# A transformer block's dense expert gates in groups of eight expert tiles: the shape of one DRAM buffer

## The chip, the cores and the metric

The kernel runs on one core of a Trainium2 chip. The metric is the device time of one execution in microseconds (us); less is better. Engines: PE is TensorE (matmuls; PEld its weight loads), DVE is VectorE, ACT ScalarE, POOL GpSimd, SP SyncE. SP, ACT and POOL issue DMA transfers, each on a queue of its own (in the trace: q1 is SP's, q10 is ACT's, q0 POOL's gathers); all queues share the core's 16 DMA engines.

## The reference

One layer of a streaming encoder: 512 frames and 16 meta tokens, model width 1024, a layer norm, a joint projection, two mixers (sparse attention and an RWKV-7 scan), their gated join, and then PEER, the part that the change touches:

```python
q = (xf @ wq).reshape(n, PEER_HEADS, 2, PEER_HALF)
s = jnp.einsum('nhpd,hpkd->nhpk', q, subkeys)          # 8 heads, 2 halves, 128 keys each
s_top, i_top = lax.top_k(s, 16)
cand = s_top[:, :, 0, :, None] + s_top[:, :, 1, None, :]
best_s, best_j = lax.top_k(cand.reshape(n, PEER_HEADS, -1), 16)
expert = ...                                            # one of 128 * 128 experts for each pick
gate = jax.nn.softmax(best_s, axis=-1)
h = jnp.einsum('nd,nhkd->nhk', xb, u[eb])               # per token: 128 picked rows of u
coef = gb * jax.nn.gelu(h, approximate=False)
out = jnp.einsum('nhk,nhkd->nd', coef, v[eb])           # and of v
```

## The kernel before

The 16,384 experts are 128 tiles of 128. For 384 of the 512 tokens (`DENSE`) PEER is computed densely: all experts' activations `gelu(u x)`, times a dense gate matrix that is zero where an expert was not picked, times `v`. The other 128 tokens are done by gathers: POOL fetches 128 rows of `u` and 128 of `v` for each token (`gather_rows`, q0), and DVE takes dot products (`dot_rows`, L1552) and sums (`add_rows`, L1561), a few after each expert tile, by a fixed table `used_by`.

Work goes in this order on every engine:

1. Queries, scores and top-k, with expert tiles of `u` between them. Each tile of `u` is loaded by SP, split by ACT into a high part (L1855) and by DVE or POOL into the rest, multiplied on PE (`tile`, L1921 and L1925), passed through gelu by ACT (L1826) and, for the first 102 tiles (`PARKED`), stored to DRAM (`parked`, q10).
2. 24 lots (`LOTS`) of 16 tokens. In each lot PE runs two expert tiles and four groups of four tokens (`four`): one-hot matrices built by DVE, multiplied on PE (L1979), give the dense gates of four tokens for all 128 x 128 experts. ACT copies them (L1870) into `lot`, a buffer of two slots of 8 KB a partition: expert within the tile on the partition, then expert tile, then token. When four copies are there, SP stores the lot to `dense_gates` (L1758) and then issues the loads of the two weight tiles after the next (L1727).
3. Six more tiles (`BEHIND`), with no lots. Then SP waits until both of the last stores have landed (L1761), issues the first gates load (L1736), four loads of parked tiles (L1743), and the first three tiles of `v`.
4. For each expert tile k of 128: DVE multiplies the activations by the gates (`weigh`, L2170), ACT and DVE split the product (L1891, L2174), PE adds its product with `v` (`sums`, L2006). The first 102 activations are read back from `parked`; the last 26 are computed here from `u` (`hidden`). A gates load brings the gates of eight expert tiles (`LOOP`) into one of two slots; there are 16. Load 1 is issued at k = 1, load i + 1 at k = 8i + 5, once the first eight products of the slot have been read (`weighed`).
5. The last layer norm, by DVE, and the output.

SP issues its transfers in the order of the code, and they stand in one queue in that order: behind a store, the weight loads; behind a gates load, a parked tile and tiles of `v`. PE has two banks for the tiles' results in stages 2 and 3, so a gelu that is late holds up the tile after the next.

In the kernel before, `dense_gates` has the shape lot, partition, and 2048 numbers (expert tile and token). A store writes one lot, 8 KB a partition, in one piece. A gates load takes, for each partition and each of the 24 lots, 128 numbers (eight tiles by 16 tokens), 512 bytes.

Of the kernel before, what the change touches and what calls it, by code (L numbers as in the profile page):

```python
# [18 lines left out]
F32 = mybir.dt.float32  # L19
# [7 lines left out]
P = 128  # L27
# [14 lines left out]
EXPERT_KEYS, PEER_HEADS, PEER_TOPK = 128, 8, 16  # L42
LOT = 16
# [3 lines left out]
LOTS = DENSE // LOT  # L47
BETWEEN = 16
PARKED = 4 * PEER_HEADS + BETWEEN + 2 * LOTS + 6
GATHER_RING = 8  # L50
MARK, FILL, LOW = -3.4e38, -3.3e38, -1.0e30


# [63 lines left out]
def build(nc, a, out):  # L117

    with ExitStack() as ctx:
        def sb(name, shape, dt=F32, at=None):  # L120
            return (at or ctx).enter_context(nc.sbuf_tensor(name, shape, dt))

        def semaphore(name, at=None):
            return (at or ctx).enter_context(nc.semaphore(name))

        ps = ctx.enter_context(nc.psum_tensor("ps", [P, 8, 512], F32))
        params = sb("params", [P, NPARAM])
        ident = sb("ident", [P, P])
        ones = sb("ones", [P, P])
        pair_ones = sb("pair_ones", [P, P])  # L130
        h_tok = sb("h_tok", [P, NT, D])
        wi_tok = sb("wi_tok", [P, NT, HEADS])
        h1T = sb("h1T", [P, KD, SEQ])[:, :, :]

        flat_h1T = h1T.rearrange("p k t -> p (k t)")
        barred = [flat_h1T[:, 2 * D + sum(WIDTH[:i]):2 * D + sum(WIDTH[:i + 1])] for i in range(NT)]
        eps = sb("eps", [P, 4])

        dense = nc.dram_tensor("dense_gates", [LOTS, P, P * LOT], F32, kind="Internal").ap()
        gates_dram = nc.dram_tensor("branch_gates", [2 * KD, P, SEQ], F32, kind="Internal").ap()  # L140
        parked = nc.dram_tensor("parked_gelu", [PARKED, P, DENSE], F32, kind="Internal").ap()

        def par(name, i=0, rows=P):
            c = PCOL[name] + i
            return params[0:rows, c:c + 1]

        with ExitStack() as layer:

            arena = sb("arena", [P, CT_GATE * PW], at=layer)
            p_all = arena[:, :].rearrange("p (c t) -> p c t", c=CT_GATE)  # L150
            ab = sb("ab", [P, 2 * PAIRS, T], at=layer)
            out_gate = sb("out_gate", [P, PAIRS, T], at=layer)
            bonus = sb("bonus", [P, PAIRS, T], at=layer)
            chunk_decay = sb("chunk_decay", [P, PAIRS, 1 + SEQ // CHUNK], at=layer)
            attended_raw = sb("attended", [P, PAIRS * T], at=layer)[:, :]
            attended = attended_raw[:, 0:PAIRS * SEQ].rearrange("p (c t) -> p c t", c=PAIRS)
            masks = sb("masks", [P, 7, CHUNK], at=layer)
            project(nc, a, locals())
            attend(nc, a, locals())
            w_pa = sb("w_pa", [P, PAIRS, D], at=layer)  # L160
            scan_chunks(nc, a, locals())
            join(nc, a, locals())
        gather_sem = semaphores(nc, ctx, "gather")
        h_hl = sb("h_hl", [P, 2, KD, SEQ], F32R)
        rows_g = sb("gathered_rows", [P, GATHER_RING, D])
        gathering = {"rows": rows_g, "index": sb("pick_index", [P, PICKS], U32), "gate": sb("pick_gate", [P, PICKS]),
                     "hidden": sb("pick_hidden", [P, PICKS]), "picked": gather_sem("picked"), "used": gather_sem("used"),
                     "landed": [gather_sem(f"landed{j}") for j in range(GATHER_RING)]}
        peer(nc, a, locals(), out)


# [1363 lines left out]
def gather_rows(nc, pool, a, gathering, n):  # L1535

    slot = n % GATHER_RING
    if n >= GATHER_RING:
        pool.wait_ge(gathering["used"], n - GATHER_RING + 1)
    table = a["u_rows"] if n < PICKS else a["v"].rearrange("k p d -> (k p) d")  # L1540
# [24 lines left out]
def peer(nc, a, g, out):  # L1565


    ps, ident, h1T, h_hl, dense, parked = g["ps"], g["ident"], g["h1T"], g["h_hl"], g["dense"], g["parked"]
# [13 lines left out]
    RING = 4  # L1582
    BY_POOL = FIRST_LOT
    DEEP = 2 * RING
    LOOP, COEFS, HLS = 8, 4, 3
    TILES_D = DENSE // P
    FRESH = EXPERT_KEYS - PARKED
    LEAD = 2
# [53 lines left out]
    with ExitStack() as ctx:  # L1642
# [33 lines left out]
        with ExitStack() as second:  # L1676
            lot = sb("lot", [P, 2, P, LOT], at=second)
# [3 lines left out]
        with ExitStack() as third:  # L1681
            gates = sb("gates", [P, 2, LOTS, LOOP * LOT], at=third)
# [21 lines left out]
        lot_stored = [sem(f"lot_stored{j}") for j in range(2)]  # L1704
# [10 lines left out]
        @block.sync  # L1715
        def _(sp):
            def load(s, j):
                sp.dma_start(staged[:, j % RING, :], a["stream"][s]).then_inc(landed[j % RING], 16)

            def load_late(s):  # L1720

                j = place_of(s)
                if j < RING:
                    sp.wait_ge(late_low, before_in_place(s) - BY_POOL + 1)
                elif s >= QUERIES + PARKED + DEEP:
                    sp.wait_ge(late_low, s - DEEP - BY_POOL + 1)
                sp.dma_start(stage[j], source(s) if s >= QUERIES + PARKED else a["stream"][s]).then_inc(landed[j], 16)  # L1727

            def load_from(first, end):
                for s in range(first, min(end, STREAMED)):  # L1730
                    load_late(s)

            def load_gates(i):
                if i >= 2:
                    sp.wait_ge(weighed, LOOP * (i - 1))
                sp.dma_start(gates[:, i % 2], dense[:, :, LOOP * LOT * i:LOOP * LOT * (i + 1)].rearrange("l p k -> p l k")  # L1736
                             ).then_inc(gates_landed[i % 2], 16)

            def load_parked(k):
                if k >= COEFS:  # L1740
                    sp.wait_ge(coef_low, k - COEFS + 1)
                sp.wait_ge(act_parked[k % 2], 16 * (k // 2 + 2))
                sp.dma_start(coef[k % COEFS], parked[k]).then_inc(act_landed[k % COEFS], 16)  # L1743

            for j in range(RING):
                load(j, j)
            sp.dma_start(g_row, a["ln1_g"].partition_broadcast(P)).then_inc(rows_landed, 16)
            sp.dma_start(b_row, a["ln1_b"].partition_broadcast(P)).then_inc(rows_landed, 16)
            sp.dma_start(sub_keys[:, :, :], a["sub_keys"]).then_inc(keys_landed, 16)
            with sp.Fori(0, BY_POOL // 8) as i:  # L1750
                for j in range(8):
                    sp.wait_ge(w_low, i * 8 + (j + 1))
                    load(i * 8 + (j + RING), j)
            for n in range(LOTS):
                first = FIRST_LOT + TILES_A_LOT * n + RING
                load_from(first, min(first + TILES_A_LOT, QUERIES + PARKED))
                sp.wait_ge(four_copied, 4 * (n + 1))
                sp.dma_start(dense[n], lot[:, n % 2, :, :].rearrange("p k n -> p (k n)")).then_inc(lot_stored[n % 2], 16)  # L1758
            load_from(FIRST_BEHIND + RING, QUERIES + PARKED)
            for j in range(2):  # L1760
                sp.wait_ge(lot_stored[j], 16 * (LOTS // 2))  # L1761
            load_gates(0)
            for k in range(COEFS):
                load_parked(k)

            load_from(QUERIES + PARKED, QUERIES + PARKED + 3)
            for j in range(2):
                sp.wait_ge(act_parked[j], 16 * (PARKED // 2 + 1))
            load_from(QUERIES + PARKED + 3, QUERIES + PARKED + DEEP)
            for k in range(EXPERT_KEYS):  # L1770
                if k + LEAD in U_AT:
                    load_from(U_AT[k + LEAD] + DEEP, U_AT[k + LEAD] + DEEP + 1)
                load_from(V_AT[k] + DEEP, V_AT[k] + DEEP + 1)
                if k == 1:
                    load_gates(1)
                if k % LOOP == LOOP - 3 and LOOP < k < EXPERT_KEYS - LOOP:
                    load_gates(k // LOOP + 1)
                if k + COEFS < PARKED:
                    load_parked(k + COEFS)
            sp.wait_ge(late_low, STREAMED - BY_POOL)  # L1780
            sp.dma_start(g2_row, a["ln2_g"].partition_broadcast(P)).then_inc(row_landed, 16)
            sp.dma_start(b2_row, a["ln2_b"].partition_broadcast(P)).then_inc(row_landed, 16)
            for t in range(NT):
                sp.wait_ge(ready, t + 1)
                sp.dma_start(out[0, P * t:P * (t + 1), :], h_tok[:, t, :]).then_inc(stored, 16)
            sp.wait_ge(stored, 16 * NT)
# [499 lines left out]
```

## Time and profile before

| | |
|---|---|
| three executions | 2085.87, 2084.53, 2076.84 us, median 2084.53 |
| profiled execution | 2081.93 us, its span 2080.2 us |
| granted TensorE clock, mean | 0.957 of full speed |
| busy, share of the span | PE 92%, DVE 74%, ACT 37%, POOL 28% |
| DMA | 416.53 MB in 173,719 packets, 200 GB/s on average |
| `dense_gates` stores | 24 of 1024 KB, issued from 1080.4 to 1338.7 us |
| gates loads | 16 of 1536 KB, issued from 1344.1 to 1954.7 us |

All times in the trace are from the span's start. The span is a little shorter than the execution's time, which also holds what lies around it. Busy shares over the whole span mix stages with different limits; the rows further down are therefore taken by stretches. The DMA share is the mean busy share of the 16 DMA engines; it can pass 1.00 a little, since a packet's time overlaps with its neighbour's. A packet is one contiguous piece.

### The profile page before, as it was taken

How to read it: one execution, taken by the hardware profiler on the slowest of the kernel's cores; microseconds unless marked ns; L12 is line 12 of the kernel's file. 1: busy time of each engine (PE TensorE's matmuls, PEld its weight loads, DVE VectorE, ACT ScalarE, POOL GpSimd, SP SyncE). 2: the span in 40 equal slices, each digit the busy share in tenths (PEclk: the TensorE clock that was granted, in tenths of full speed). 3: DMA queues.
4: the chain of work that ended last, by engine and by line, in shares of the span. 5: the costliest groups of instructions: out<-in, count | busy, mean ns of one | idle time of the engine just before them, and what ended most of it. 6: DMA issues, size and time to landing. Idle time of an engine off the chain costs nothing.

```text
span 2080.2 us, 34092 instructions
## 1 busy us (share of the span) xinstructions
PE 1909.4 (92%) x13250; PEld 1617.5 (78%) x13250; DVE 1537.8 (74%) x2826; ACT 761.0 (37%) x1113; POOL 581.0 (28%) x403
## 2 busy tenths in 40 slices
PE   5989998789999879999999999969999999999892
PEld 4968876348974359999999999958888788888782
DVE  6277993314545269999978888748877788799998
ACT  3222554532210033333446666523333333332320
POOL 2322343000000035555531011222222222266661
PEclk9988998897999999999999999989999999999997
DMA  3211232010023034344567777899999999999994
GB/s 124 71 61 47 86 111 71 0 42 3 4 79 126 0 146 138 131 132 134 172 234 277 267 272 267 307 322 361 339 364 344 345 346 349 312 356 389 382 347 152
DMA packets 173719, 416.53 MB, mean 200 GB/s; under 512 B 13952, under 2 KB 89216, under 8 KB 170384
## 3 DMA queue, kind: packets, MB, share of 16 engines
q1 hardware_dynamic: 119728, 256.16, 36.0%
q0 software_dynamic: 36864, 134.23, 17.2%
q10 hardware_dynamic: 16992, 24.26, 3.2%
q8 instruction: 95, 1.56, 0.3%
q14 instruction: 40, 0.33, 0.1%
HBM read 363.08 MB, written 51.51 MB: 199 GB/s over the span
## 4 chain that ended last, share of the span: by engine, by line
PE 34%; DVE 24%; DMA 4%; issue 2%; SPq 0%; ACT 0%; DVEq 0%; ACTq 0%
PE ps L2006 18%; PE ps L1921 8%; DVE h_tok L1561 7%; PE ps L1925 4%; PE ps L1979 3%; DVE w_hl L2144 2%; DVE is_place L2088 2%; DVE is_place L2083 1%; DVE picks L2091 1%; DVE top_at L2049 1%; DVE top_at L2058 1%; DVE s_head L2052 1%; DMA coef<-parked_gelu 1%; DMA gates<-dense_gates 1%; DMA h1T<-in_v 1%
## 5 line engine op out<-in xcount | busy, mean ns | idle before, releaser
L2006 PE MATMUL ps<-w_hl,coef_hl 128*128 128x512 f32 x2304 | 539.1, 394 | 28.3 <-DVE coef_hl L2174 28.3
L2006 PEld LDWEIGHTS ps<-w_hl,coef_hl 128*128 128x128 f32 x2304 | 432.9, 189 | 130.5 <-DVE coef_hl L2174 37.0
L1921 PE MATMUL ps<-h_hl,w_hl 128*128 128x384 f32 (+1 forms) x2304 | 446.6, 345 | 19.9 <-ACT h1T L1826 11.1
L1921 PEld LDWEIGHTS ps<-h_hl,w_hl 128*128 128x128 f32 x2304 | 406.4, 189 | 33.2 <-ACT w_hl L1855 11.4
L1542 POOL DMA_INDIRECT gathered_rows<-in_u_rows,pick_index x128 | 137.5, 1074 | 538.2 <-DVE pick_hidden L1552 529.2
L1925 PE MATMUL ps<-h_hl,w_hl 128*128 128x384 f32 (+1 forms) x1152 | 230.0, 340 | 0.0
L1855 ACT ACTIVATE w_hl<-w_staged 128x1024 fp32r<-128x1024 f32 x143 | 152.0, 1063 | 188.9 <-PE ps L2006 137.2
L1925 PEld LDWEIGHTS ps<-h_hl,w_hl 128*128 128x128 f32 x1152 | 203.4, 188 | 5.0
L1542 POOL DMA_INDIRECT gathered_rows<-in_v,pick_index x128 | 164.8, 1288 | 148.4 <-DVE h_tok L1561 97.9
L1795 POOL TENSOR_TENSOR w_hl<-w_staged,w_hl 128x1024 fp32r<-128x1024 f32 x64 | 163.7, 2561 | 135.5 <-ACT w_hl L1820 111.1
L1561 DVE SCALAR_TENSOR_TENSOR h_tok<-gathered_rows,pick_hidden,h_tok 128x1024 f32<-128x1024 f32 x128 | 164.1, 1282 | 10.0 <-DVE h_tok L1561 0.5
L632 PE MATMUL ps<-hT_hl,w_hl 128*128 128x264 f32 (+1 forms) x1024 | 168.1, 323 | 0.0
L2144 DVE TENSOR_TENSOR w_hl<-w_staged,w_hl 128x1024 fp32r<-128x1024 f32 x130 | 157.8, 1218 | 11.2 <-ACT w_hl L1855 11.2
L297 POOL TENSOR_TENSOR w_hl<-w_staged,w_hl 128x1024 fp32r<-128x1024 f32 x40 | 102.8, 2571 | 213.6 <-ACT w_hl L480 213.6
L632 PEld LDWEIGHTS ps<-hT_hl,w_hl 128*128 128x128 f32 x1024 | 150.6, 198 | 14.4 <-issue 2.8
L1552 DVE CUSTOM_DVE_ANT_0 gathered_rows<-gathered_rows,h_tok 128x1024 f32<-128x1024 f32 x128 | 155.4, 1217 | 0.0
L1855 ACT ACTIVATE w_hl<-h1T 128x1024 fp32r<-128x1024 f32 x78 | 82.9, 1063 | 169.2 <-PE ps L2006 125.8
L2174 DVE TENSOR_TENSOR coef_hl<-coef,coef_hl 128x384 fp32r<-128x384 f32 x128 | 71.2, 556 | 73.4 <-ACT coef_hl L1891 73.1
L1891 ACT ACTIVATE coef_hl<-coef 128x384 fp32r<-128x384 f32 x128 | 65.6, 513 | 142.1 <-DVE coef L2170 141.7
L1790 POOL IOTA count<- 128x16 f32 x1 | 0.1, 148 | 397.7 <-POOLq L111 397.7
L1826 ACT ACTIVATE h1T<-ps 128x384 f32<-128x384 f32 x102 | 50.0, 491 | 155.9 <-PE ps L1925 152.1
L2144 DVE TENSOR_TENSOR w_hl<-h1T,w_hl 128x1024 fp32r<-128x1024 f32 x78 | 94.5, 1217 | 16.4 <-ACT w_hl L1855 16.4
(315 smaller groups left out, 2546.8 us busy)
## 6 DMA issues: line engine op xcount, KB each, us to landing
w_staged<-in_stream SPq DMA_DIRECT2D x132, 512.0 KB
h1T<-in_v SPq DMA_DIRECT2D x66, 512.0 KB
w_staged<-in_v SPq DMA_DIRECT2D x62, 512.0 KB
dense_gates<-lot SPq DMA_DIRECT2D x24, 1024.0 KB
gates<-dense_gates SPq DMA_DIRECT2D x16, 1536.0 KB
w_staged<-in_w_in_t SPq DMA_DIRECT2D x40, 512.0 KB
parked_gelu<-h1T ACTq DMA_DIRECT2D x102, 192.0 KB
coef<-parked_gelu SPq DMA_DIRECT2D x102, 192.0 KB
```

Of the source, the lines that this page charges most:

```text
L297: nc.gpsimd.tensor_tensor(w_hl[:, j, 1, :], w_staged[:, j, :], w_hl[:, j, 0, :].bitcast(F32), ALU.subtract).then_inc(w_low, 1)
L632: nc.tensor.matmul(banks[b], w_hl[:, j, 0, P * k:P * (k + 1)], hT_hl[:, part, k, lo:hi], start=(k == 0 and part == 0), stop=False)
L1542: nc.gpsimd.indirect_dma_start(gathering["rows"][:, slot, :], None, table, bass.IndirectOffsetOnAxis(gathering["index"][:, column:column + ...
L1552: nc.vector.tensor_tensor_reduce(rows, rows, h_tok[:, 0, :], 1.0, 0.0, ALU.mult, ALU.add, gathering["hidden"][:, n:n + 1]).then_inc(gather ...
L1561: nc.vector.scalar_tensor_tensor(h_tok[:, 0, :], gathering["rows"][:, slot, :], gathering["hidden"][:, pick:pick + 1], h_tok[:, 0, :], ALU ...
L1795: nc.gpsimd.tensor_tensor(w_hl[:, j % RING, 1, :], staged[:, j % RING, :], w_hl[:, j % RING, 0, :].bitcast(F32), ALU.subtract).then_inc(w_ ...
L1855: nc.scalar.activation(w_hl[:, s % RING, 0, :], stage[place_of(s)], ACT.Copy).then_inc(w_high, 1)
L1921: nc.tensor.matmul(ps[:, bank, 0:width], w_hl[:, j % RING, 0, P * k:P * (k + 1)], h_hl[:, part, k, lo:SEQ], start=(k == 0 and part == 0), ...
L1925: last = nc.tensor.matmul(ps[:, bank, 0:width], w_hl[:, j % RING, 1, P * k:P * (k + 1)], h_hl[:, 0, k, lo:SEQ], start=False, stop=(k == KD ...
L2006: last = nc.tensor.matmul(ps[:, 2 + 2 * t + half, :], coef_hl[:, k % HLS, c, P * t:P * (t + 1)], w_hl[:, s % RING, v, 512 * half:512 * (ha ...
L2144: v_.tensor_tensor(w_hl[:, s % RING, 1, :], stage[place_of(s)], w_hl[:, s % RING, 0, :].bitcast(F32), ALU.subtract).then_inc(late_low, 1)
L2174: v_.tensor_tensor(coef_hl[:, k % HLS, 1, :], coef[k % COEFS], coef_hl[:, k % HLS, 0, :].bitcast(F32), ALU.subtract).then_inc(coef_low, 1)
```

## The change

The buffer `dense_gates` gets another shape: group of eight expert tiles, partition, lot, and 8 x 16 numbers. A gates load then reads 24 x 128 numbers, 12 KB, in one piece for each partition. A store writes a lot as 16 pieces of 512 bytes for each partition, 1.5 MiB apart in DRAM; in SBUF its source stays as it is. Sizes, the order of instructions on every engine, waits and semaphores are the same; `LOOP` keeps its value of 8 and is now named by a constant of the module.

```diff
+GATE_TILES = 8
...
-        dense = nc.dram_tensor("dense_gates", [LOTS, P, P * LOT], F32, kind="Internal").ap()
+        dense = nc.dram_tensor("dense_gates", [EXPERT_KEYS // GATE_TILES, P, LOTS, GATE_TILES * LOT], F32, kind="Internal").ap()
...
-    LOOP, COEFS, HLS = 8, 4, 3
+    LOOP, COEFS, HLS = GATE_TILES, 4, 3
...
             def load_gates(i):
                 if i >= 2:
                     sp.wait_ge(weighed, LOOP * (i - 1))
-                sp.dma_start(gates[:, i % 2], dense[:, :, LOOP * LOT * i:LOOP * LOT * (i + 1)].rearrange("l p k -> p l k")
+                sp.dma_start(gates[:, i % 2], dense[i]
                              ).then_inc(gates_landed[i % 2], 16)
...
                 sp.wait_ge(four_copied, 4 * (n + 1))
-                sp.dma_start(dense[n], lot[:, n % 2, :, :].rearrange("p k n -> p (k n)")).then_inc(lot_stored[n % 2], 16)
+                sp.dma_start(dense[:, :, n, :].rearrange("g p c -> p g c"),
+                             lot[:, n % 2, :, :].rearrange("p (g k) n -> p g (k n)", k=LOOP)).then_inc(lot_stored[n % 2], 16)
```

## Rows read from the trace of the kernel before

**Rows 1.** The page: busy time of the engines, and the chain that ended last.
```profile
PE 1909.4 (92%) x13250; PEld 1617.5 (78%) x13250; DVE 1537.8 (74%) x2826; ACT 761.0 (37%) x1113; POOL 581.0 (28%) x403
...
PE 34%; DVE 24%; DMA 4%; issue 2%; SPq 0%; ACT 0%; DVEq 0%; ACTq 0%
```

**Rows 2.** Stretches: us, busy of PE, PEld, DVE, ACT, POOL, PEclk, DMA share, GB/s.
```profile
1080.00:1339.00 259.00, 259.00 (x2214) 251.77 (x2213) 225.09 (x368) 159.84 (x186) 30.43 (x26) 1.00 0.78 271
1344.00:1360.00 16.00, 13.91 (x81) 13.59 (x79) 6.94 (x10) 2.88 (x4) 6.46 (x5) 1.00 1.06 370
1360.00:1372.00 12.00, 2.96 (x9) 2.99 (x10) 3.45 (x6) 3.60 (x5) 0.81 (x1) 0.60 0.84 315
1372.00:1400.00 28.00, 21.12 (x86) 17.06 (x86) 16.51 (x27) 7.34 (x11) 6.22 (x6) 0.93 0.89 303
1440.00:1480.00 40.00, 40.00 (x177) 32.81 (x176) 31.47 (x48) 13.59 (x20) 9.69 (x10) 1.00 1.00 351
1860.00:1920.00 60.00, 55.57 (x272) 48.40 (x272) 57.70 (x56) 19.54 (x27) 37.78 (x29) 1.00 1.02 380
```

**Rows 3.** PE's timeline: start, duration, engine, line, tiles, count [idle before <- releaser].
```profile
1353.58 2.93 PE L1921 MATMUL ps<-h_hl,w_hl 128*128 128x384 f32 x16
...
1369.04 4.67 PE L1921 MATMUL ps<-h_hl,w_hl 128*128 128x384 f32 x16 [11.13 <-ACT h1T L1826]
...
1386.39 18.55 PE L2006 MATMUL ps<-w_hl,coef_hl 128*128 128x512 f32 x72 [4.77 <-DVE coef_hl L2174]
1405.45 6.92 PE L2006 MATMUL ps<-w_hl,coef_hl 128*128 128x512 f32 x29 [0.51 <-DVE coef_hl L2174]
...
1649.91 2.34 PE L2006 MATMUL ps<-w_hl,coef_hl 128*128 128x512 f32 x9 [1.09 <-DVE coef_hl L2174]
```

**Rows 4.** ACT's timeline, same columns, 1340 to 1390 us.
```profile
1367.46 1.06 ACT L1855 ACTIVATE w_hl<-h1T 128x1024 fp32r<-128x1024 f32 x1 [15.94 <-DMA h1T<-in_v]
1368.43 0.47 ACT L1826 ACTIVATE h1T<-ps 128x384 f32<-128x384 f32 x1
```

**Rows 5.** SP's queue in order of time, 1320 to 1420 us.
```profile
1327.40 0.33 SPq L1758 DMA_DIRECT2D dense_gates<-lot  x1
...
1338.66 0.33 SPq L1758 DMA_DIRECT2D dense_gates<-lot  x1
...
1344.15 0.38 SPq L1736 DMA_DIRECT2D gates<-dense_gates  x1
1344.57 11.94 SPq L1743 DMA_DIRECT2D coef<-parked_gelu  x4
1356.55 23.69 SPq L1727 DMA_DIRECT2D h1T<-in_v  x4
```

**Rows 6.** DMA queue 1, 1354 to 1356 us: packets, MB, share of 16 engines.
```profile
q1 hardware_dynamic: 1097, 0.56, 108.8%
```

**Rows 7.** DMA queue 1, 1366 to 1368 us.
```profile
q1 hardware_dynamic: 221, 0.82, 102.7%
```

**Rows 8.** DMA packets in all, by size, and queue 1, 1283 to 1287 us.
```profile
DMA packets 173, 1.17 MB, mean 292 GB/s; under 512 B 16, under 2 KB 16, under 8 KB 45
...
q1 hardware_dynamic: 173, 1.17, 95.0%
```

**Rows 9.** DMA queue 10 (parked tiles' stores), 1370 to 1372 us.
```profile
q10 hardware_dynamic: 163, 0.23, 32.0%
```

**Rows 10.** ACT's rows in the timeline, 1282 to 1312 us.
```profile
1300.47 1.06 ACT L1855 ACTIVATE w_hl<-w_staged 128x1024 fp32r<-128x1024 f32 x1 [1.17 <-DMA w_staged<-in_stream]
...
1302.01 0.49 ACT L1826 ACTIVATE h1T<-ps 128x384 f32<-128x384 f32 x1 [0.48 <-PE ps L1925]
```

**Rows 11.** DMA queue 0 (the gathers), 1348 to 1352 us.
```profile
q0 software_dynamic: 349, 1.27, 78.2%
```

**Rows 12.** DMA queues 0 and 1, 1360 to 1362 us.
```profile
q0 software_dynamic: 180, 0.63, 81.6%
q1 hardware_dynamic: 182, 0.16, 23.2%
```

## The prediction

> **What bounds the kernel now.** The order of reading is: the page's totals and its chain of waits, the stretches, and then, where TensorE (PE) stands still, the timelines of the engines and the DMA queues. The span is 2080.2 us and PE is busy for 92% of it; the chain ends on PE and VectorE (DVE) lines, and DMA holds 4% of it [rows 1]. That small share is all that a change of transfers alone can reach directly, so the question is where it lies. The stretches tell [rows 2]. While the dense gates are made and stored (1080 to 1339 us) PE is busy all the time, and the 16 DMA engines for 0.78 of it. From 1400 to about 1800 PE is full too (40.00 of 40), although DMA stands at 1.00. From 1860 on DVE is the bound (57.70 of 60 us) and PE merely waits for it. Only 1344 to 1405 us holds an open stall: PE works 13.91 of 16, 2.96 of 12 and 21.12 of 28 us.
>
> The PE timeline names these stalls [rows 3]: 11.13 us before the tile at 1369.04, 4.77 before the sums at 1386.39, 0.51 at 1405.45, and one later of 1.09 at 1649.91, while a gates load is awaited. Behind the first is ScalarE (ACT), which waits 15.94 us for the first tile of `in_v` and only then, at 1368.43, can apply the gelu that frees PE's bank [rows 4]. Behind that is SyncE's (SP's) queue [rows 5]: the last store of dense gates is issued at 1338.66, the first gates load at 1344.15, when both store semaphores are up, then four loads of parked tiles, whose issue takes 11.94 us in all, and so the first `in_v` load leaves at 1356.55. Its bytes are behind the whole gates load in one queue.
>
> **The change, part by part.** No instruction is added, removed or moved on any engine. Each of 16 gates loads goes from 3,072 pieces of 512 bytes to 128 pieces of 12 KB; each of 24 stores goes from 128 pieces of 8 KB to 2,048 of 512 bytes. All transfers use 16 DMA engines, so per engine a load falls from 192 pieces to 8, and a store rises from 8 to 128.
>
> *Price of a load.* In 1354 to 1356 only gates pieces run on queue 1: 1,097 packets take 108.8% of 2 us on 16 engines, 34.8 engine-us, 31.7 ns for one [rows 6]. A load costs 192 x 31.7 = 6.1 us of all engines. A 4 KB piece costs, from 1366 to 1368, 32.9 engine-us for 0.82 MB, about 200 pieces, 0.164 us [rows 7]; a 12 KB piece at this rate is 0.49 us and the load 8 x 0.49 = 3.9 us. The saving is 2.1 us of DMA a load.
>
> *Price of a store.* From 1283 to 1287 one store and the start of a weight load take 95.0% of 4 us on 16 engines, 60.8 engine-us, for 1.17 MB [rows 8]. Of its packets 45 are under 8 KB and 16 of these under 512 bytes, so 29 are weight pieces of 4 KB; at 0.164 us each [rows 7] they leave 0.44 us for each of the 128 pieces, 8 x 0.44 = 3.5 us a store. The trace has no write of 512 bytes to memory. Bounds: a 512-byte read, 31.7 ns [rows 6], makes 128 x 31.7 = 4.1 us; the parked tiles' writes of 1,536 bytes, which take 32.0% of 2 us on 16 engines, 10.2 engine-us, for 0.23 MB, about 150 pieces, so 68 ns each [rows 9], make 8.7 us. At the other side a rate as that of large pieces, 20 ns for 512 bytes, would make 2.6 us, a gain of 0.9. I take 4.1, since the read has the same size and the written 1,536 bytes cost hardly more per byte than a 4 KB read. So a store costs 0.6 us more.
>
> *What the stores cost.* In a lot of 11.26 us (from 1327.40 to 1338.66 [rows 5]) DMA is busy for 0.78, which leaves 2.5 us; 0.6 fits. Behind the store in the queue stand two weight loads, and ACT waits 1.17 us for the first of them; the gelu behind it has still 0.48 us in hand before PE's tile is ready, and the bank it frees is wanted only by the tile after the next, over 5 us later [rows 10]. A delay of 0.6 us costs nothing; what hides it is this spare bank, and were it gone, 24 x 0.6 = 14 us would show. The last store has no such cover: the gates load waits for it, and all behind moves by 0.6 us.
>
> *What the loads gain.* At 1344 to 1368: 2.1 us less in front of the `in_v` tile, less 0.6 from the late store, is 1.5 us. Turns matter too: when the gathers (queue 0) compete, from 1348 to 1352 they hold 78.2% of the engines [rows 11], and from 1360 to 1362 the queues pass as many packets (180 and 182) while queue 0 holds 81.6% of the time [rows 12]. So a queue with 512-byte pieces gets small turns, and with 12 KB pieces large ones. But the turns won in the gates load are given back: the four parked loads after it have pieces of 1,536 bytes (32 turns an engine, each against a gather piece of 0.17 us), and the gathers put off then run beside them. Of 8 turns of the `in_v` tile itself perhaps half a microsecond is won. I take 2.0 us for the first stall. The 4.77 us stall follows it one to one, as it waits for the parked gelus of the same tiles, and keeps its length. The stall of 0.51 us (a parked load behind the second gates load) and that of 1.09 us go: 1.6 us. The other gates loads lie beside full PE or beside a full DVE and give nothing. Sum: 2.0 + 1.6 = 3.6 us. Bounds of the first stall's gain: from -3.1 us (the last store at 8.7 us, 5.2 late, less the 2.1) to all of 11.13.
>
> The profiled execution took 2081.93 us, its sum 2078.3; it lies 2.6 us under the median of 2084.53, from which the same sum gives **2080.9**. A measurement of this kernel can tell about 0.5%, 10.4 us, from no change, and 3.6 us is well inside: I forecast no difference that shows.
>
> **Rivals.** *The stall disappears.* If queue 1 gets far more turns than counted, or the parked loads are issued so much sooner that the gathers fall behind them, the `in_v` tile is there 11 us earlier. Then 11.13 us go, and with it the slow start after it: the 16 matmuls at 1369.04 take 4.67 us where a running PE takes 2.93 for the same (the granted clock was 0.60 in this stretch [rows 2], against 1.00 elsewhere), 1.7 us. With the 1.6 us above: 14.4 us, 2070.1 us. For it: SP's issue is held up 11.94 us by the many pieces [rows 5]. Against it: the bytes before the tile stay, and the engines are busy for 1.06 and 0.84 of the stretches before it [rows 2].
>
> *The stores become the bound.* If a written piece costs more than (3.5 + 2.5) / 128 = 47 ns, a lot has more DMA work than its 11.2 us, the weights come late, and PE waits in all 24 lots. At the upper bound of 68 ns it is 8.7 - 6.0 = 2.7 us a lot, 65 us in all, 2150 us. For it: the profile shows no such small write, and 1,536 bytes already took 68 ns. Against it: time per packet grows with bytes in every row.
> A rule speaks for this rival. In this trace the old loads, whose successive pieces lie 1 MiB apart, already move 512 bytes in 31.7 ns [rows 6], against 20 ns for 512 bytes at the rate of 4 KB pieces [rows 7]; which part of the 11 ns is the small piece's and which the distance's, no row tells. The Trainium skill (DMA: Bandwidth & Descriptors, section on latency and other measured facts) reports that copies between tensors with a row pitch of a large power of two fall from 207 to 164 GB/s at 2 MiB and to 103 at 4 MiB; the new stores step 1.5 MiB between a partition's pieces. The trace has no such halving at its 1 MiB step. If a new piece took twice the 31.7 ns, by the same working, it would be 8.1 us a store, 2.1 us over, 50 us in all and 2135 us; I give this cause 0.04 of the 0.10 below.
>
> *All is hidden.* The gathers take up what the loads release, and the store's delay eats the rest: 2084.5 us. It differs from my forecast in size only. That the pieces are cut smaller than 12 KB is possible too and ends at the same place.
>
> **How the numbers follow.** Forecast of a few microseconds: 0.52. Nothing at all: 0.16. The stall gone or most of it: 0.22. Slow stores: 0.10. The first two are within 0.5%; of the third nearly all counts as faster, a part of it, where only half the stall goes, does not. Thus faster 0.21, within 0.5% 0.69, slower 0.10. The range goes from 2067 (the stall gone from a median as shown, and 3 us for the runs' own spread) to 2091 (no gain, a late store, and the spread of the runs); the slow stores are outside it.
>
> **What would show it.** Right: a gates load that holds the engines for about 3.9 us, not 6.1; lots still 11.2 us apart; PE full to 1339 us; the stall near 1369 about 9 us long; no stall at a gates load. The first rival: that stall under 3 us and a clock of 1.00. The second: PE stalls in the lots with ACT waiting for `w_staged`, DMA at 1.0 from 1080 to 1339. Wrong outright: a change of the time after 1860 us, where I count none.

## The result, and the profile after

The changed kernel takes 2139.32 us (median of 4, 2135.93 to 2140.72) against 2083.34 us: a ratio of 1.0271, 95% interval 1.0244 to 1.0299. The prediction, 2080.9 us with a range of 2067 to 2091 and 0.69 on "within 0.5%", is wrong. It is slower by 56 us, where the forecast saw 3.6 us of gain.

The page after, in the lines that answer to [rows 1], and its packets:

```profile
PE 1940.8 (91%) x13250; PEld 1636.7 (77%) x13250; DVE 1537.4 (72%) x2826; ACT 756.9 (35%) x1113; POOL 578.5 (27%) x403
...
DMA packets 172695, 416.53 MB, mean 195 GB/s; under 512 B 13952, under 2 KB 89216, under 8 KB 170384
...
PE 27%; DVE 23%; DMA 8%; issue 3%; ACT 2%; SPq 0%; ACTq 0%; DVEq 0%
```

The bytes are the same, and the count of packets hardly differs: what the loads lost in small pieces the stores gained. DMA's part of the chain has doubled from 4% to 8%.

The spans differ by 58.8 us. Laid out by the stores of dense gates: the first store is issued at 1087.74 us, 7.3 later than before; the 24 stores take 303.9 us from first to last (before: 1080.42 to 1338.66, 258.2), 45.6 more; and from the last store to the end it is 747.4 us (741.5), 5.9 more. The first part is not put down to the change: nothing ahead of the first store differs, and in the other profiled executions its time runs from 1075.3 to 1085.6. The last part is not put down to late transfers either. Its main row on PE, before and after:

```profile
L2006 PE MATMUL ps<-w_hl,coef_hl 128*128 128x512 f32 x2304 | 539.1, 394 | 28.3 <-DVE coef_hl L2174 28.3
```

```profile
L2009 PE MATMUL ps<-w_hl,coef_hl 128*128 128x512 f32 x2304 | 547.4, 399 | 27.1 <-DVE coef_hl L2177 27.1
```

The same 2,304 matmuls take 8.3 us more, though PE waits no longer than before and the granted clock is 1.00 in the steady stage of both. Run 3 below has the same transfers in this stage, and there they take 539.0 us, so the new shape of the buffer does not do it; why this execution was slower there stays open. What is the change's is the loss in the lots, 45.6 us of the 56.

Stretches of the kernel after, in the columns of [rows 2]:

```profile
1088.00:1146.00 58.00, 58.00 (x493) 56.43 (x492) 50.63 (x83) 33.98 (x40) 5.67 (x5) 1.00 0.80 261
1146.00:1392.00 246.00, 217.63 (x1741) 209.48 (x1741) 173.74 (x283) 121.48 (x145) 20.50 (x21) 0.95 0.70 226
...
1460.00:1500.00 40.00, 40.00 (x173) 32.42 (x172) 31.98 (x50) 13.29 (x18) 9.52 (x10) 1.00 0.94 331
...
1920.00:1980.00 60.00, 55.52 (x270) 48.19 (x269) 57.60 (x56) 18.95 (x26) 37.70 (x29) 1.00 1.00 393
```

For the first five lots PE is still full. Then it stands still for 28 of 246 us. Its work there also takes some 14 us more than at the pace before (1,741 matmuls in 217.63 us, where 2,214 took 259.00): the granted clock was 0.95 in this stretch, where it was 1.00. These two are most of the 45.6 us. And the DMA engines are busy for less of the time (0.70) than before the change (0.78), so they have time to spare. The later stages are as forecast but for the slower matmuls: PE full, DMA down from 1.00 to 0.94, and DVE the bound at the end, 57.60 of 60 us.

Who waits in the lots, 1088 to 1392 us (engine, line, releaser: us in total, times, longest):

```profile
ACT w_hl L1858 <- DMA w_staged<-in_stream: 122.9, 23, 7.2
PE ps L1924 <- ACT h1T L1829: 28.4, 15, 4.0
```

ACT waits once a lot for weights, 5.3 us on average, where it waited about 1 us. Two lots in SP's queue, an early and a late one:

```profile
1099.11 0.38 SPq L1760 DMA_DIRECT2D dense_gates<-lot  x1
...
1110.76 0.38 SPq L1760 DMA_DIRECT2D dense_gates<-lot  x1
...
1282.61 0.38 SPq L1760 DMA_DIRECT2D dense_gates<-lot  x1
1283.04 3.07 SPq L1729 DMA_DIRECT2D w_staged<-in_stream  x2
1296.01 0.38 SPq L1760 DMA_DIRECT2D dense_gates<-lot  x1
```

and the same two lots on ACT:

```profile
1106.85 1.06 ACT L1858 ACTIVATE w_hl<-w_staged 128x1024 fp32r<-128x1024 f32 x1 [2.31 <-DMA w_staged<-in_stream]
...
1292.11 1.06 ACT L1858 ACTIVATE w_hl<-w_staged 128x1024 fp32r<-128x1024 f32 x1 [5.86 <-DMA w_staged<-in_stream]
1293.08 0.47 ACT L1829 ACTIVATE h1T<-ps 128x384 f32<-128x384 f32 x1
...
1293.96 2.02 ACT L1873 ACTIVATE lot<-ps 128x512 f32<-128x512 f32 x2 [0.41 <-ACT h1T L1829]
```

Read the late lot as a circle: store at 1282.61, the two weight loads behind it in the same queue, the first of them in ACT's hands at 1292.11 (9.5 us after the store), then ACT's split, gelu and two copies, and with the fourth copy the next store, at 1296.01 (3.9 us). A lot takes 9.5 + 3.9 = 13.4 us, whatever PE could do. This sum holds in every lot of the changed kernel: the first part goes from 7.5 to 10.8 us, and the next store is issued 3.9 us after it each time. Before the change the first part was 6.2 to 6.9 us (6.75 in the lot of [rows 10], whose store was issued at 1293.72), so the circle needed 10.1 to 10.8 us and PE's pace of 11.2 ruled. The first part may be 11.2 - 3.9 = 7.3 us long. In the early lot it is 7.7.

PE in the late lot, with its stall, and the same sixteen matmuls when PE had not stood still (4.58 us against 3.02; seven of the 15 stalls were followed by such slow ones):

```profile
1293.69 4.58 PE L1924 MATMUL ps<-h_hl,w_hl 128*128 128x384 f32 x16 [1.96 <-ACT h1T L1829]
...
1300.86 3.02 PE L1924 MATMUL ps<-h_hl,w_hl 128*128 128x384 f32 x16
```

### The profile page after: what moved, and what is told of

It is laid out like the page before. It is cut to its first block, busy times and chain, and to the rows that moved or that the text cites. A ratio compares the mean times of both kernels' runs of the same rounds, so it can differ in the third digit from the quotient of the medians.

```text
span 2139.0 us, 34092 instructions
## 1 busy us (share of the span) xinstructions
PE 1940.8 (91%) x13250; PEld 1636.7 (77%) x13250; DVE 1537.4 (72%) x2826; ACT 756.9 (35%) x1113; POOL 578.5 (27%) x403
## 4 chain that ended last, share of the span: by engine, by line
PE 27%; DVE 23%; DMA 8%; issue 3%; ACT 2%; SPq 0%; ACTq 0%; DVEq 0%
PE ps L2009 20%; DMA w_staged<-in_stream 7%; DVE h_tok L1563 7%; PE ps L1924 4%; DVE w_hl L2147 2%; PE ps L1928 2%; DVE is_place L2091 1%; DVE is_place L2086 1%; DMA h1T<-in_v 1%; PE ps L1982 1%; ACT lot L1873 1%; DVE picks L2094 1%; DVE top_at L2052 1%; DVE top_at L2061 1%; DVE s_head L2055 1%
## 5 line engine op out<-in xcount | busy, mean ns | idle before, releaser
L2009 PE MATMUL ps<-w_hl,coef_hl 128*128 128x512 f32 x2304 | 547.4, 399 | 27.1 <-DVE coef_hl L2177 27.1
L1924 PE MATMUL ps<-h_hl,w_hl 128*128 128x384 f32 (+1 forms) x2304 | 459.5, 352 | 48.5 <-ACT h1T L1829 39.7
L1924 PEld LDWEIGHTS ps<-h_hl,w_hl 128*128 128x128 f32 x2304 | 418.5, 195 | 65.2 <-ACT w_hl L1858 42.7
L1928 PE MATMUL ps<-h_hl,w_hl 128*128 128x384 f32 (+1 forms) x1152 | 230.1, 340 | 0.0
L1928 PEld LDWEIGHTS ps<-h_hl,w_hl 128*128 128x128 f32 x1152 | 203.6, 188 | 5.0
L1563 DVE SCALAR_TENSOR_TENSOR h_tok<-gathered_rows,pick_hidden,h_tok 128x1024 f32<-128x1024 f32 x128 | 164.2, 1283 | 10.0 <-DVE h_tok L1563 0.5
L2147 DVE TENSOR_TENSOR w_hl<-h1T,w_hl 128x1024 fp32r<-128x1024 f32 x78 | 94.6, 1219 | 13.7 <-ACT w_hl L1858 13.7
L1873 ACT ACTIVATE lot<-ps 128x512 f32<-128x512 f32 x96 | 97.0, 1117 | 20.0 <-ACT h1T L1829 14.5
```

The costliest lines, as they stand in the source:

```text
L1563: nc.vector.scalar_tensor_tensor(h_tok[:, 0, :], gathering["rows"][:, slot, :], gathering["hidden"][:, pick:pick + 1], h_tok[:, 0, :], ALU ...
L1873: nc.scalar.activation(lot[:, n % 2, :, FOUR * q:FOUR * (q + 1)].rearrange("p k n -> p n k"), ps[:, 4 + q, :].rearrange("p (n k) -> p n k" ...
L1924: nc.tensor.matmul(ps[:, bank, 0:width], w_hl[:, j % RING, 0, P * k:P * (k + 1)], h_hl[:, part, k, lo:SEQ], start=(k == 0 and part == 0), ...
L1928: last = nc.tensor.matmul(ps[:, bank, 0:width], w_hl[:, j % RING, 1, P * k:P * (k + 1)], h_hl[:, 0, k, lo:SEQ], start=False, stop=(k == KD ...
L2009: last = nc.tensor.matmul(ps[:, 2 + 2 * t + half, :], coef_hl[:, k % HLS, c, P * t:P * (t + 1)], w_hl[:, s % RING, v, 512 * half:512 * (ha ...
L2147: v_.tensor_tensor(w_hl[:, s % RING, 1, :], stage[place_of(s)], w_hl[:, s % RING, 0, :].bitcast(F32), ALU.subtract).then_inc(late_low, 1)
```

## Experiments

The theories that went in. **A**: the circle just read. **B**: the distance of 1.5 MiB between a partition's pieces makes the writes slow. **C**: the DMA engines have no time left in a lot, the rival on record. Ratios are to the kernel before on the same chip.

**1. Small pieces both ways, stored side by side.**

```diff
-        dense = nc.dram_tensor("dense_gates", [EXPERT_KEYS // GATE_TILES, P, LOTS, GATE_TILES * LOT], ...)
+        dense = nc.dram_tensor("dense_gates", [EXPERT_KEYS // GATE_TILES, LOTS, P, GATE_TILES * LOT], ...)
...
-                sp.dma_start(gates[:, i % 2], dense[i]
+                sp.dma_start(gates[:, i % 2], dense[i].rearrange("l p c -> p l c")
...
-                sp.dma_start(dense[:, :, n, :].rearrange("g p c -> p g c"),
+                sp.dma_start(dense[:, n, :, :].rearrange("g p c -> p g c"),
```

> Stores in 512-byte pieces as in the change, but their pieces for neighbouring partitions lie side by side in 64 KB blocks, and the gates loads are back at 512-byte pieces. Theory A (a circle: a lot's store stands in SP's queue ahead of the two weight loads; ACT waits for the first of these before its gelu and the copies that release the next store): nothing changes in the lots, periods of 13.3 to 13.8 us, total 2130 to 2145. Theory B (the 1.5 MiB between a partition's pieces makes the writes slow): the distance is gone, so the lots come back to 11.3 us and the total to 2080 to 2090. Theory C (the 16 DMA engines have no time left in a lot): as A here.

Measured: 2127.58 us, ratio 1.0227 (1.0188 to 1.0267). First to last store 302.5 us, against 303.9. B falls: it asked for 2080 to 2090. The total is 2.4 us under the range of A and C (2130 to 2145); the lots start at 11.4 us, are over 13 from the eighth on and reach 14.9. Its ratio is 0.0044 under the changed kernel's, some 9 us, with nearly the same time in the lots; the slower matmuls read above are as large, and here they take 539.5 us. The price of the distance, too, can be read: queue 1 in 1283 to 1287 us, first of the changed kernel, where only store pieces run, then of this one:

```profile
q1 hardware_dynamic: 1752, 0.90, 80.9%
```

```profile
q1 hardware_dynamic: 699, 0.36, 30.8%
```

The share times 16 engines times 4 us gives 51.8 engine-us for 1,752 packets, 29.6 ns each, and 19.7 for 699, 28.2 ns. Here a 512-byte write costs about as much as the 512-byte read of [rows 6] (31.7 ns), near or far.

**2. Large pieces both ways.** The loads read 12 KB runs of the old buffer, which hold gates of other experts and tokens; the right gates are left out, the work is the same.

```diff
+            by_load = dense.rearrange("l p k -> (l p k)").rearrange("(i p c) -> i p c", p=P, c=LOTS * LOOP * LOT)
...
-                sp.dma_start(gates[:, i % 2], dense[:, :, LOOP * LOT * i:LOOP * LOT * (i + 1)].rearrange("l p k -> p l k")
+                sp.dma_start(gates[:, i % 2].rearrange("p l k -> p (l k)"), by_load[i]
```

> Stores of 8 KB a partition as before, and gates loads of 12 KB a partition from the same buffer; DVE multiplies by gates that belong to other experts and tokens. It measures the loads' half of the change alone. A, B and C all say that the lots stay at 11.26 us; the record's sum gives the loads 5.6 us before the late store is taken off (4.1 at the first stall, 1.6 at the two small ones at most), so 2076 to 2083. If 12 KB pieces themselves do harm by holding up gathers and weights, over 2087.

Measured: 2075.85 us, ratio 0.9974 (0.9954 to 0.9994). The lots stay at 11.2 us, and from the last store to the end it takes 736.1 us instead of 741.5: 5.4 us. The expectation had 2076 to 2083. The sum on record without its late store is 2.0 + 0.6 + 1.6 = 4.2 us (the expectation added it up wrongly, to 5.6). The loads' half of the change is of the sign and size that was forecast; the loss in the lots comes with the stores. The parts of the sum are not those forecast:

```profile
1363.96 5.46 PE L1923 MATMUL ps<-h_hl,w_hl 128*128 128x384 f32 x16 [7.62 <-ACT h1T L1828]
...
1379.80 16.76 PE L2008 MATMUL ps<-w_hl,coef_hl 128*128 128x512 f32 x72 [0.66 <-DVE coef_hl L2176]
1398.84 21.35 PE L2008 MATMUL ps<-w_hl,coef_hl 128*128 128x512 f32 x92 [2.27 <-DVE coef_hl L2176]
```

The first stall is 3.5 us shorter, the one of 4.77 us, which was to stay, has 0.66 left, the one of 0.51 us, which was to go, is 2.27, and the matmuls behind the first stall are slower than before.

**3. The weights ahead of the store.** Only SP's order changes: the two loads that used to be issued right behind a store are issued right ahead of it. Pieces and bytes stay those of the changed kernel.

```diff
+            load_from(FIRST_LOT + RING, FIRST_LOT + RING + TILES_A_LOT)
             for n in range(LOTS):
...
-                load_from(first, min(first + TILES_A_LOT, QUERIES + PARKED))
                 sp.wait_ge(four_copied, 4 * (n + 1))
+                load_from(first + TILES_A_LOT, first + 2 * TILES_A_LOT)
                 sp.dma_start(dense[:, :, n, :].rearrange("g p c -> p g c"),
...
-            load_from(FIRST_BEHIND + RING, QUERIES + PARKED)
```

> The changed kernel, but SP issues the two weight loads ahead of the lot's store, not behind it; the same pieces and bytes. A: the circle is cut, lots 11.2 to 11.4 us, PE full to the end of the lots, total 2074 to 2086. B and C: the writes take as long and the engines have the same work, so the lots stay at 13 us or more, total over 2125.

Measured: 2078.92 us, ratio 0.9978 (0.9955 to 1.0001). The stretch of its lots:

```profile
1078.00:1337.00 259.00, 259.00 (x2215) 251.77 (x2214) 224.52 (x367) 156.16 (x184) 32.14 (x27) 1.00 0.84 273
```

PE is full, with the same small pieces and more DMA work in the same time (0.84). A had 2074 to 2086, B and C over 2125. This carries the verdict: A holds, and C is out. The slower store does harm only where the awaited loads stand behind it.

**4. Each lot stored twice, in large pieces, in the kernel before.**

```diff
                 sp.dma_start(dense[n], lot[:, n % 2, :, :].rearrange("p k n -> p (k n)")).then_inc(lot_stored[n % 2], 16)
+                sp.dma_start(again[n % 2], lot[:, n % 2, :, :].rearrange("p k n -> p (k n)")).then_inc(lot_stored[n % 2], 16)
```

(the waits on `lot_stored` count twice as far; `again` is a new DRAM buffer that nothing reads.)

> The kernel before, each lot stored twice in 8 KB pieces, the second time to a buffer that nothing reads. No small piece anywhere. A: the weights land 3.5 us later, a period of 6.4 + 3.5 + 3.9 = 13.8 us once the slack is used, total 2125 to 2145. C: DMA work of 0.78 * 11.26 + 3.5 = 12.3 us a lot, 24 * 1.0 = 25 us, total 2105 to 2112. B, or any theory in which the small pieces as such do the harm: 2082 to 2090.

Measured: 2172.76 us, ratio 1.0428 (1.0389 to 1.0467); a miss on the far side of A, 28 us over its range. No piece is small, and the lots are the slowest of all: 14.3 to 15.7 us from the third on, the last but one 16.4. From SP's and ACT's timelines and the stretch of its lots:

```profile
1304.14 0.33 SPq L1759 DMA_DIRECT2D dense_gates<-lot  x1
```

```profile
1314.59 1.06 ACT L1857 ACTIVATE w_hl<-w_staged 128x1024 fp32r<-128x1024 f32 x1 [6.82 <-DMA w_staged<-in_stream]
```

```profile
1084.00:1423.00 339.00, 283.01 (x2232) 272.54 (x2231) 224.34 (x367) 154.40 (x185) 24.75 (x25) 0.94 0.75 280
```

The first part is 10.4 us in this lot, and 10.4 + 3.9 is 14.3. The circle is there without small pieces. But the weights came later than the 3.5 us added: A lacked something, which is run 5's question.

**5. No gathers in the lots.** In the changed kernel the gather's issue moves against the store from lot to lot. POOL's timeline, an early and a late lot (stores at 1099.11 and 1282.61):

```profile
1102.44 1.13 POOL L1544 DMA_INDIRECT gathered_rows<-in_u_rows,pick_index  x1 [10.09 <-DVE pick_hidden L1554]
```

```profile
1282.45 0.94 POOL L1544 DMA_INDIRECT gathered_rows<-in_u_rows,pick_index  x1 [12.39 <-DVE pick_hidden L1554]
```

```diff
                 low(BY_POOL + TILES_A_LOT * (n + 1))
-                dot_rows(nc, dve, h_tok, gathering, n)
...
-    used_behind = [LOTS + 2 * (n + 1) for n in range(BEHIND)]
+    used_behind = [2 * (n + 1) for n in range(BEHIND)]
```

> The changed kernel without DVE's dot products of gathered rows during the 24 lots, so that no gather runs there; their 24 rows are moved to the expert tiles after the parked ones, and the end of the kernel gets longer by about 24 * 1.3 = 31 us. Only the lots count here. A, with the gather as what feeds the circle (it keeps its own clock, the store drifts late, and the gather's 4 KB pieces then take turns against 512-byte pieces and stand in front of the weights): without it a lot takes 6.4 + 1.2 + 3.9 = 11.5 us at most, last store less first store 258 to 266 us against 304. If the small store alone is slow enough: periods stay over 13 us and the difference over 295.

Measured: 2130.36 us in all, of which only the lots count: 277.5 us from first to last store. Neither figure of the record held; it lies between. Of 23 lots 19 take 11.3 to 12.1 us (the first part is 7.4 to 8.2 us), four 12.7 to 13.7; these four make some 5 us, and their cause was not looked for. So of the 45.6 us more about 19 stay when the gathers are gone, and 26 go with them. DVE's dot products (1.2 us each) go too in this run; DVE is not in the circle, but the run does not part the two. In the first lots of the changed kernel the gather is issued 3.5 us after the store; as the store drifts later, the gather comes to lie 0.2 us ahead of it, its 4 KB pieces take turns against 512-byte ones, and ACT has the weights after 9.1 to 10.8 us instead of 8. The drift feeds itself until the two are issued together.

**6. The store on ACT's queue.**

```diff
-                sp.dma_start(dense[:, :, n, :].rearrange("g p c -> p g c"), ...).then_inc(lot_stored[n % 2], 16)
...
                 copy(n, 3)
+                act.wait_ge(four_copied, 4 * (n + 1))
+                nc.scalar.dma_start(dense[:, :, n, :].rearrange("g p c -> p g c"), ...).then_inc(lot_stored[n % 2], 16)
```

> The changed kernel, but the lot's store is issued by ACT on its own queue after the fourth copy, so the weights in SP's queue take turns with it and stand behind nothing. A: periods 11.2 to 11.4 us, total 2074 to 2088. B or C: over 2125. A harm of its own that is possible: the parked tile's store now stands behind the lot's on ACT's queue; it is awaited two gelus (11 us) later, so I expect none.

Measured: 2081.50 us, ratio 1.0003 (0.9984 to 1.0021), lots at 11.2 us, PE full:

```profile
1080.00:1340.00 260.00, 260.00 (x2228) 252.76 (x2225) 226.98 (x371) 160.87 (x186) 30.70 (x26) 1.00 0.83 270
```

A second way out of the circle, with the same result for the lots. ACT no longer waits for weights in them. The first gates load is issued 14.0 us after the last store (5.5 before), as in run 3, whose end is looked at in run 8.

**7. Pieces of 1 KB.** Groups of sixteen tiles, so that a store has half the pieces; the loads read 512-byte pieces, as before.

```diff
+PIECE_TILES = 16
...
-        dense = nc.dram_tensor("dense_gates", [EXPERT_KEYS // GATE_TILES, P, LOTS, GATE_TILES * LOT], ...)
+        dense = nc.dram_tensor("dense_gates", [EXPERT_KEYS // PIECE_TILES, P, LOTS, PIECE_TILES * LOT], ...)
...
-                sp.dma_start(gates[:, i % 2], dense[i]
+                sp.dma_start(gates[:, i % 2], dense[i // 2][:, :, LOOP * LOT * (i % 2):LOOP * LOT * (i % 2 + 1)]
...
-                             lot[:, n % 2, :, :].rearrange("p (g k) n -> p g (k n)", k=LOOP)).then_inc(lot_stored[n % 2], 16)
+                             lot[:, n % 2, :, :].rearrange("p (g k) n -> p g (k n)", k=PIECE_TILES)).then_inc(lot_stored[n % 2], 16)
```

> The changed kernel with groups of sixteen tiles: a store has 8 pieces of 1 KB a partition, a gates load reads 24 pieces of 512 bytes a partition. A store's bare time falls from 4.1 us to about 3.4 at 64 pieces of some 45 to 50 ns an engine. A: the excess of the weights' landing over the 7.6 us that the circle allows gets smaller and builds up later; periods of 11.2 to 12.6 us, first to last store 260 to 285 us, total 2085 to 2120. If only the count of bytes a piece under 1 KB matters: 258 us, 2083.

Measured: 2078.58 us, ratio 0.9982 (0.9965 to 0.9999); all lots 11.2 us, first to last store 258.2. This misses the figures that A gave (260 to 285 us, a total of 2085 to 2120); the lots are those of the other expectation (258 us). A's forecast had the weights over the limit of the circle, and they stayed under it. How little was left is in ACT's timeline in one lot (store issued at 1288.57):

```profile
1295.63 1.06 ACT L1859 ACTIVATE w_hl<-w_staged 128x1024 fp32r<-128x1024 f32 x1 [1.48 <-DMA w_staged<-in_stream]
1296.85 0.49 ACT L1830 ACTIVATE h1T<-ps 128x384 f32<-128x384 f32 x1 [0.15 <-PE ps L1929]
```

The weights are there after 7.1 us (6.9 to 7.3 in the lots but the last), and the gelu has 0.15 us in hand, where it had 0.48 [rows 10]. At 7.1 us the circle still closes inside 11.2; at 7.5, in the first lots of the changed kernel, it does not. So the result fits a circle with a limit of 7.3 us; it does not by itself rule out that 1 KB pieces are harmless for another reason.

**8. The end of the lots.** In run 3 the last store stands behind the last weights, and the first gates load waits for it: issue at 1336.65 and 1351.61.

```profile
1336.65 0.48 SPq L1761 DMA_DIRECT2D dense_gates<-lot  x1
1351.61 0.33 SPq L1738 DMA_DIRECT2D gates<-dense_gates  x1
```

Two versions follow. The first gives the last lot its old order:

```diff
-                load_from(first + TILES_A_LOT, first + 2 * TILES_A_LOT)
+                if n < LOTS - 1:
+                    load_from(first + TILES_A_LOT, first + 2 * TILES_A_LOT)
...
+            load_from(FIRST_BEHIND + RING, QUERIES + PARKED)
             for j in range(2):
                 sp.wait_ge(lot_stored[j], 16 * (LOTS // 2))
```

> As weights_first, but in the last lot the store goes ahead of the last two weight loads again, since there it is the store that is awaited (15.0 us from its issue to the first gates load in weights_first, 5.5 in the kernel before). If that wait is what the boundary lost: the gates load is issued 6 to 9 us sooner, the stall of 11.9 us before the tile at 1366 falls to 6 to 8 us, total 2070 to 2077. If the gathers take all of it: as weights_first, 2079.

The second moves the `in_v` tiles too:

```diff
+            load_from(QUERIES + PARKED, QUERIES + PARKED + 3)
             for j in range(2):
                 sp.wait_ge(lot_stored[j], 16 * (LOTS // 2))
             load_gates(0)
             for k in range(COEFS):
                 load_parked(k)
-            load_from(QUERIES + PARKED, QUERIES + PARKED + 3)
```

> As last_store_first, and the first three tiles of in_v are loaded ahead of the first gates load and the parked tiles, not behind them. If the stall at the end of the lots is the in_v tile's place behind 2.3 MB in one queue: it falls to under 2 us, with the cold clock after it (1.5 us), and what is late next is the gates load with the first parked tile, needed some 20 us later; total 2062 to 2070. If the DMA engines' work as such sets it, the stall moves to the first product of gates and activations and the total stays at 2070 to 2077.

Measured: 2076.47 us (0.9977, 0.9960 to 0.9994) and 2073.46 us (0.9954, 0.9937 to 0.9971). In the first the total is inside its 2070 to 2077, by another way than forecast: the gates load is issued 12.7 us after the last store instead of 15.0, where 6 to 9 us less were forecast; the stall before the `in_v` tile falls to 1.27 us, and one of 4.50 us comes before it, at the lots' own weights. The second is the fastest version of the study, with an interval clear of the kernel before. It is short of its 2062 to 2070; its total is in the range that the other expectation gave, in which the work of the DMA engines only moves the stall (2070 to 2077). Its two main stalls on PE:

```profile
1354.29 5.14 PE L1926 MATMUL ps<-h_hl,w_hl 128*128 128x384 f32 x16 [4.69 <-ACT h1T L1831]
...
1372.45 5.99 PE L2011 MATMUL ps<-w_hl,coef_hl 128*128 128x512 f32 x18 [3.29 <-DVE coef_hl L2179]
```

The 11 us stall is gone, and what is late next is a weight tile of the lots' own (ACT waits 10.90 us for it) and then the first product.

**9. The two reorderings in the old layout.** Run 3's edit, and the second edit of run 8 alone, in the kernel before.

> The kernel before with the one reordering of weights_first: SP issues the two weight loads ahead of the lot's store. The old layout's circle has room, so its lots stay at 11.2 us, and at the end the store is awaited longer: 2083 to 2090, that is the same or a little slower than before. It tells how much of weights_first (2078.9) is the layout's: 4 to 8 us if the large gates reads are worth what large_both showed.

> The kernel before, with the first three tiles of in_v loaded ahead of the gates load and the parked tiles. If the stall of 11.13 us is the in_v tile's place in the queue, it falls to under 5 us and the first product of gates and activations is late instead, since the gates load in 512-byte pieces now starts 4 us later and loses its turns against the gathers: total 2076 to 2082. If the work of the engines sets it: 2082 to 2086.

Measured: 2088.01 us, ratio 1.0023 (1.0005 to 1.0041), and 2078.53 us, ratio 0.9975 (0.9954 to 0.9996). The stall that the `in_v` tile had caused, in the first and in the second:

```profile
1376.84 4.48 PE L1921 MATMUL ps<-h_hl,w_hl 128*128 128x384 f32 x16 [14.62 <-ACT h1T L1826]
```

```profile
1376.38 43.90 PE L2006 MATMUL ps<-w_hl,coef_hl 128*128 128x512 f32 x184 [13.77 <-DVE coef_hl L2174]
```

In the first it is longer, since the store is awaited longer. In the second the tile waits no more and the whole wait has moved to the first product; the profiled span is nevertheless 7.1 us shorter, and the two later stalls of the kernel before (2.1 and 4.77 us) are gone; what is left of the 7.1 us was not taken apart. Weights first gains nothing in a layout whose circle has room. With the circle cut, the changed layout stands at 0.9978 and the old one at 1.0023 of the kernel before: 0.45%, some 9 us, with intervals that do not meet, is what the new layout is worth in this order. Against the best order of each layout less is left: 0.9954 for the new (run 8) and 0.9975 for the old (`in_v` first), 0.2% or some 4 us, with intervals that overlap.

## Why the prediction was wrong

*What bounds the kernel, and the later stages.* Right. The steady stage stayed full, if at the slower matmuls of that execution; the 10 waits of DVE for gates loads between 1410 and 1800 us are gone, and the stall at 1649.91 with them; at the end DVE is still the bound.

*Price of a load.* Right: 3.9 us was forecast. In the changed kernel from 1404 to 1406 us:

```profile
q1 hardware_dynamic: 51, 0.63, 74.0%
q0 software_dynamic: 52, 0.21, 26.2%
```

23.7 engine-us for 51 pieces are 0.46 us, 3.7 us a load. The turns, one piece against one, are in the same rows: queue 1 now holds three quarters of the engines.

*Price of a written piece.* Right: 31.7 ns was taken, 29.6 ns measured; the bound of 68 ns was far off.

*What the stores cost.* Here the step failed: "A delay of 0.6 us costs nothing; what hides it is this spare bank". The spare bank does hide a gelu that is late once. But ACT's next work behind that gelu is the copies that release the next store, and the next weights stand behind that store. The delay comes round again, and every lot adds to it. The row held the warning: 0.48 us in hand [rows 10] was the slack of a circle. By the limit of 7.3 us the slack was 0.4 to 1.1 us over the 24 lots, 0.7 on average, so that a delay of 0.6 would have used it up and 1.0 went over it; the 1 KB pieces, with 0.5 us later weights, cost nothing. So a size was off as well. The weights came 1.0 us later in the first lots, not 0.6 (7.5 to 7.8 us against 6.6 on average), and 3 us later once the gather had come in front. The trace shows this delay in the store itself. In windows of a quarter of a microsecond, the old store has its last piece under way 3.9 us after its issue (lot of 1293.72 us), and the new one at 5.1 us (lot of 1110.76), with the weights' pieces taking over at these times. By engine time the difference is only 0.3 us (128 x 29.6 ns = 3.8 against the 3.5 taken for the old one): the new store's pieces thin out towards its end, from about 143 in a window to under 80, so its end comes later than the sum of its pieces says. Engine time is not landing time: what counts is everything that stands ahead of the awaited load in its queue, with the turns that other queues take meanwhile.

*The rival of slow stores* named the right place and its range of 2135 to 2150 us holds the result, but by the wrong mechanism. It needed a piece over 47 ns and a DMA share of 1.0. The piece cost 29.6 ns and the share fell to 0.70. That its number fits is chance. It had 0.10.

*What would show it* did its work: "PE stalls in the lots with ACT waiting for `w_staged`" was to be seen at once; "DMA at 1.0" was not, and that separated A from C before any run.

*The first stall.* From the first gates load's issue to the `in_v` tile in ACT's hands it was 23.3 us before (1344.15 to 1367.46 [rows 4, 5]). After:

```profile
1397.59 0.33 SPq L1738 DMA_DIRECT2D gates<-dense_gates  x1
1397.96 2.31 SPq L1745 DMA_DIRECT2D coef<-parked_gelu  x4
1400.31 31.74 SPq L1729 DMA_DIRECT2D h1T<-in_v  x4
```

```profile
1419.36 1.06 ACT L1858 ACTIVATE w_hl<-h1T 128x1024 fp32r<-128x1024 f32 x1 [13.64 <-DMA h1T<-in_v]
```

21.8 us: 1.5 us sooner, where the prediction took 2.1 for the load and 0.5 for the turns. The gates load itself is issued 6.0 us after the last store instead of 5.5, the late store that was put at 0.6. Together the tile is 1.0 us sooner after the last store, where 2.0 were taken. SP's four parked loads are issued in 2.31 us instead of 11.94, and that is worth nothing, as argued against the first rival. The stall behind the tile falls from 11.13 to 7.51 us, but most of that is only moved: the lots' late weights leave a new stall of 3.88 us ahead of it.

```profile
1403.31 4.58 PE L1924 MATMUL ps<-h_hl,w_hl 128*128 128x384 f32 x16 [3.88 <-ACT h1T L1829]
...
1420.94 4.46 PE L1924 MATMUL ps<-h_hl,w_hl 128*128 128x384 f32 x16 [7.51 <-ACT h1T L1829]
```

So PE's stalls from the last store to 1440 us add up to 18.6 us, and those at the same place before to 18.5. In run 2, without late weights, 5.4 us were gained.

## What to carry to other kernels

When a transfer gets slower, do not price it by the engines' time alone. List what stands behind it in its queue, follow who waits for that, and go on until the path either ends or comes back to the transfer itself; if it comes back, the slack is what is left of the period, and any delay above it is paid in every turn of the loop, growing until the buffers are used up. The cheap remedy is the order of issue: loads that are awaited first, a store that nobody awaits last, or the store on another queue. And where the last of such stores is awaited, its place has to be looked at by itself.

## What was not expected of the hardware

- The size of a piece matters, its distance from the next one does not at these strides: 512-byte writes took 29.6 ns with 1.5 MiB between a partition's pieces and 28.2 ns with neighbouring partitions side by side. No run here shows the loss at wide strides on which the prediction had put 0.04.
- A loop with two clocks in it can drift. The gather kept the pace of DVE and the store that of its circle, so their distance went from 3.5 us to -0.2 us over seven lots, and with it the time to the weights from 7.5 us to 9.1 to 10.8. Without the gather the same stores cost less than half as much.
- The size of the pieces is not what decides here but how late it makes the load behind them: twice the stores in 8 KB pieces cost 89 us, single stores in 512-byte pieces 56 us (45.6 of them in the lots), and in 1 KB pieces nothing.
- The same matmuls need not take the same time at the same granted clock. In 220 us of the steady stage, with PE full and the clock at 1.00, the profiled execution of the changed kernel did 945 matmuls (1579 to 1799 us), and that of run 3, with the same transfers, 963 (1517 to 1737 us). Why stays open.
